# Four pairs of gate projections by Strassen's seven products in the second mixer, and two attention units to a block

## The chip, the cores and the metric

The kernel runs on one core of one Trainium2 chip. The metric is the device time of one execution in microseconds (us). Engines are called by their names in the profile: PE (matmuls), DVE (VectorE), ACT (ScalarE), POOL (GpSimd, which here mostly issues DMAs) and SP (which only issues DMAs).

## The reference, cut to what matters

Two transformer blocks follow each other on one sequence of 1024 tokens with 1024 channels. All arithmetic is float32. The change is in the first half of the second block:

```python
h = _rmsnorm(x, g_mix_pre)
proj = h @ w_in + b_in                      # 1024 -> 512 + 512 + 128 + 128 + 2048
u_pool, q, k, v, gates = jnp.split(proj, IN_SPLITS_2, axis=-1)
y_pool = _multiscale_pool(u_pool, w_pool, pool_scale)      # windows 2, 4, 8, 16
q, k = rotary on the first 16 of 64 channels of each head
y_attn = sliding-window attention with sinks (8 query heads, 2 key heads, window 128)
g = sigmoid(gates)                          # two gates of 1024 channels
merged = g_pool * (y_pool @ w_branch_pool) + g_attn * (y_attn @ w_branch_attn)
x = x + _rmsnorm(merged @ w_out, g_mix_post)
```

## The kernel before

Activations lie with channels on the 128 partitions and the 1024 tokens along the row. A projection is worked off in blocks: one block is 128 output channels, that is 8 slices of input channels, 2 halves of the tokens and 3 matmuls of 128x512 each, 48 matmuls in all. The three matmuls stand for one float32 product: operand and weight are each split into a high part in the fast float32 form (`fp32r`) and a low part, and high x high, low x high and high x low are added.

The input projection of the second mixer is 26 blocks, numbered by `d` (block `B_WIN2 + d`): first ten for queries, keys, values and pooling input, in the order `QKV_FIRST = (4, 5, 6, 7, 8, 9, 0, 1, 2, 3)` (four tiles of queries, one of keys, one of values, four for pooling), then the 16 gate blocks. The loops are written out by hand, one for each engine, and semaphores tie them. For each block:

- SP loads the weights into one of two slots of `w_stage`; ACT writes the high part `w_hi` (`next_high`, line L956); DVE writes the low part `w_lo` (`next_low`, L1729). Both are done in block `d` for block `d + 1`. PE waits for `w_lo` and for the evacuation of the block two before (`evac_done`).
- DVE evacuates the finished block from PSUM, multiplied by the norm's root `R` (L2770 for d < 10, L2774 for gates). For d < 10, ACT then adds the bias (`qkv_bias`, L1516). A gate block goes to `T` and from there by a DMA of POOL to `g_spill` in memory.

Rotary turning needs a copy of the query and key tiles in which groups of 8 partitions are swapped. POOL clears `swq` and `swk` by memset, then issues four DMAs for the queries (`swq<-Z`, 8 partitions x 4096 each) and four for the keys (L905). DVE then turns the queries in three instructions (`turn_queries`, L2699, L2701, L2703, one each in the blocks d = 4, 5, 6) and the keys (`turn_keys`, L2707 to L2710, d = 6).

Attention is cut into 16 units `u` (`UNITS`). The even and odd units use the two halves of the PSUM banks 4 to 7 in turn. Unit `u` belongs to block `d = 8 + u`: PE makes the scores (`scores2`, L3480) in the middle of the block, DVE shifts them and takes the maximum (`shift`, L2730 to L2739), ACT takes exponentials (`weights`, L1533), DVE normalises (`normalise2`, L2748 to L2752); in the middle of the next block PE transposes the weights (`turn_weights2`, L3489), ACT copies them (`turned_out`, L1523), at that block's end PE multiplies by the values (`values2`, L3499), and ACT copies the result out (`attended`, L1543). `scores2(u)` waits until `attended(u - 2)` has emptied its bank. DVE does the pooling of four tiles in the blocks `POOL_AT`, in one piece each.

Before it takes `X` for anything else, the kernel saves it to `x_spill` (4 MB, POOL).

The first mixer of the same kernel already has four pairs of its projection by Strassen's scheme: line L3026, 28 products of 12 matmuls each, 7 for a pair of blocks (`in_pair`, `in_low`, `in_out` and so on). Its loops are the ones that the change makes common.

## Time and profile before

| | |
|---|---|
| median of 3 runs | 2448.07 us (2447.64 to 2448.21) |
| the profiled execution | 2448.01 us, of which the span 2446.2 us |
| PE busy | 2411.3 us (99%) |
| DVE busy | 1735.8 us (71%) |
| ACT busy | 1074.3 us (44%) |
| mean granted TensorE clock | 0.997 |

Busy time is that in which an engine has an instruction in work. A matmul's length is modelled and overlaps with the next, so that the distance from start to start is the price of one. DMA issues stand at the engine that issues them.

### The profile page before, as it was taken

To read this page: it belongs to the slowest core of one execution; us is meant where nothing else is said; L and a number is where in the kernel's file an instruction comes from. 1 tells how busy PE (TensorE), PEld (TensorE's weight loads), DVE (VectorE), ACT (ScalarE), POOL (GpSimd) and SP (SyncE) were. 2 spreads that over 40 slices of the span, in tenths; PEclk is the share of its full clock that TensorE was granted. 3 is DMA by queue.
4 is the path that set the end of the run, shared out by engine and by line. 5 is a ranking of instruction groups with operands and counts; after the bars stand their busy time and mean duration, and the time that the engine had idled before them with its cause. 6 is when DMAs were issued, how large, how long until landed. Compare 5 with 4: busy or idle time off the path is not lost.

```text
span 2446.2 us, 29794 instructions
## 1 busy us (share of the span) xinstructions
PE 2411.3 (99%) x11510; PEld 1920.4 (79%) x11510; DVE 1735.8 (71%) x2088; ACT 1074.3 (44%) x1549; POOL 141.4 (6%) x230
## 2 busy tenths in 40 slices
PE   8999999999999999999999999999999999999997
PEld 6877666688888888888788777788878888888885
DVE  7668766646877778798863565455588777786888
ACT  7245777625333333333642333343456333334336
POOL 1002100000000010000001000000001000100001
PEclk9999999999999999999999999999999999999999
DMA  5110000132533382500133122234344433715103
GB/s 209 53 56 23 1 1 13 66 129 104 172 104 104 113 300 95 180 1 18 61 128 121 55 70 69 70 138 148 133 150 173 171 104 112 264 38 200 41 1 138
DMA packets 76231, 252.24 MB, mean 103 GB/s; under 512 B 6304, under 2 KB 6352, under 8 KB 76064
## 3 DMA queue, kind: packets, MB, share of 16 engines
q1 hardware_dynamic: 43728, 131.08, 16.6%
q0 software_dynamic: 32368, 119.32, 13.0%
q8 instruction: 88, 1.44, 0.2%
q14 instruction: 47, 0.39, 0.0%
HBM read 186.78 MB, written 62.91 MB: 102 GB/s over the span
## 4 chain that ended last, share of the span: by engine, by line
PE 87%; DVE 8%; ACT 2%; issue 2%; DMA 0%; DVEq 0%; ACTq 0%; SPq 0%; PEldq 0%
PE ps L2952 27%; PE ps L3385 20%; PE ps L3423 18%; PE ps L3553 7%; PE ps L3026 3%; PE ps L3256 2%; PE ps L3318 1%; DVE opQ_lo L2367 1%; DVE opQ_lo L2364 1%; PE ps L3298 1%; DVE spot L2409 1%; DVE ql_raw L2404 1%; PE ps L3480 1%; PE ps L3499 1%; PE ps L3220 1%
## 5 line engine op out<-in xcount | busy, mean ns | idle before, releaser
L3423 PE MATMUL ps<-opQ_hi 128*128 128x512 f32 x896 | 350.3, 391 | 2.8 <-DVE opQ_lo L2367 2.8
L3423 PE MATMUL ps<-opQ_lo,opQ_hi 128*128 128x512 f32 x896 | 348.7, 389 | 0.0
L3423 PE MATMUL ps<-opQ_hi,opQ_lo 128*128 128x512 f32 x896 | 348.7, 389 | 0.0
L3423 PEld LDWEIGHTS ps<-opQ_hi 128*128 128x128 f32 x896 | 168.2, 188 | 42.2 <-DVE opQ_lo L2367 7.2
L3423 PEld LDWEIGHTS ps<-opQ_hi,opQ_lo 128*128 128x128 f32 x896 | 168.2, 188 | 35.1
L3423 PEld LDWEIGHTS ps<-opQ_lo,opQ_hi 128*128 128x128 f32 x896 | 168.2, 188 | 34.6 <-issue 0.2
L1385 ACT ACTIVATE opQ_hi<-spot 128x1024 fp32r<-128x1024 f32 x80 | 84.9, 1061 | 235.8 <-PE ps L3423 196.7
L3385 PE MATMUL ps<-opQ_hi,form_hi 128*128 128x512 f32 x416 | 161.8, 389 | 0.0
L3385 PE MATMUL ps<-opQ_lo,form_hi 128*128 128x512 f32 x416 | 161.8, 389 | 0.0
L3385 PE MATMUL ps<-opQ_hi,form_lo 128*128 128x512 f32 x416 | 161.8, 389 | 0.0
L2952 PE MATMUL ps<-opP_hi,w_hi 128*128 128x512 f32 x510 | 159.5, 394 | 2.3 <-DVE T L2651 0.7
L2952 PE MATMUL ps<-opP_lo,w_hi 128*128 128x512 f32 x510 | 157.1, 389 | 0.0
L2952 PE MATMUL ps<-opP_hi,w_lo 128*128 128x512 f32 x510 | 157.1, 389 | 0.0
L2952 PE MATMUL ps<-opQ_hi,w_hi 128*128 128x512 f32 x480 | 155.6, 405 | 0.0
L1729 DVE TENSOR_TENSOR w_lo<-w_stage,w_hi 128x1024 fp32r<-128x1024 f32 x96 | 117.4, 1223 | 50.8 <-ACT w_hi L956 50.1
L2364 DVE TENSOR_TENSOR opQ_lo<-spot,opQ_hi 128x1024 fp32r<-128x1024 f32 x80 | 97.9, 1223 | 74.1 <-ACT opQ_hi L1385 74.1
L2952 PE MATMUL ps<-opQ_lo,w_hi 128*128 128x512 f32 x480 | 148.6, 391 | 0.0
L2952 PE MATMUL ps<-opQ_hi,w_lo 128*128 128x512 f32 x480 | 148.1, 390 | 0.0
L956 ACT ACTIVATE w_hi<-w_stage 128x1024 fp32r<-128x1024 f32 x96 | 100.9, 1051 | 86.9 <-PE ps L2952 59.0
L3385 PE MATMUL ps<-t_hi,form_hi 128*128 128x512 f32 x312 | 121.4, 389 | 0.0
L3385 PE MATMUL ps<-t_lo,form_hi 128*128 128x512 f32 x312 | 121.4, 389 | 0.0
L3385 PE MATMUL ps<-t_hi,form_lo 128*128 128x512 f32 x312 | 121.4, 389 | 0.0
(508 smaller groups left out, 4964.7 us busy)
## 6 DMA issues: line engine op xcount, KB each, us to landing
w_stage<-in_w_stream SPq DMA_DIRECT2D x96, 512.0 KB, 3.6
h_spill<-T POOLq DMA_DIRECT2D x56, 512.0 KB, 5.0
pair_raw<-in_w_stream SPq DMA_DIRECT2D x26, 1024.0 KB, 5.8
spot<-in_w_stream SPq DMA_DIRECT2D x24, 1024.0 KB, 7.2
spot<-h_spill POOLq DMA_DIRECT2D x24, 1024.0 KB, 9.3
qh_raw<-in_w_stream SPq DMA_DIRECT2D x8, 1024.0 KB, 11.6
ql_raw<-h_spill POOLq DMA_DIRECT2D x8, 1024.0 KB, 7.7
g_spill<-T POOLq DMA_DIRECT2D x16, 512.0 KB, 2.9
```

The lines of the kernel that those rows point to most:

```text
L956: act.activation(w_hi[:, slot, :], w_stage[:, slot, :], ACT.Copy).then_inc(w_hi_done, 1)
L1385: act.activation(weight_form(opQ_hi, i), source, ACT.Copy).then_inc(ff["form"], 1)
L1729: v.tensor_tensor(w_lo[:, slot, :], w_stage[:, slot, :], w_hi[:, slot, :].bitcast(F32), ALU.subtract)\
L2364: done(v.tensor_tensor(weight_form(opQ_lo, i), weight_form(ql_raw, i) if f == Q6 else weight_part(sc, name_w, g), weight_form(opQ_hi, i).b ...
L2367: done(v.tensor_tensor(inner_form(opQ_lo, i), t2_sum[:, :, :] if f == Q6 else inner_part(sc, name_h, g), inner_form(opQ_hi, i).bitcast(F32 ...
L2404: done(v.tensor_tensor(weight_form(ql_raw, i), weight_part(sc, "D", g), weight_part(sc, "A", g), ALU.subtract))
L2952: mm = pe.matmul(ps[:, psum + half, :], weight, operand[:, k, half * HALF:(half + 1) * HALF], start=(begin and x == 0 and weight is wh and ...
L3026: mm = pe.matmul(ps[:, (4 + f) % 8, :], weight[:, wcols(k)], operand[:, k0 + k, c0:c0 + HALF], start=(k == 0 and weight is form_h and oper ...
L3256: mm = pe.matmul(ps[:, bank, 0:n], QT[0:QKD, h, qt * P:(qt + 1) * P], KT[0:QKD, h, c:c + n], start=True, stop=True)
L3385: mm = pe.matmul(ps[:, pair_bank(x, p, j), :], weight[:, wcols(k)], operand[:, k0 + k, c0:c0 + HALF], start=(k == 0 and weight is form_hi[ ...
L3423: mm = pe.matmul(ps[:, down_bank(sc, f) + m, :], weight, operand, start=(g == 0 and kt == 0 and weight is wh and operand is hi), stop=(g = ...
L3553: mm = pe.matmul(ps[:, 2 * slot + half, :], weight[:, slot, wcols(k)], operand[:, k, c], start=(k == 0 and weight is w_hi and operand is h ...
```

## The change

Eight of the 16 gate blocks are taken out of the row of blocks and made as four pairs by Strassen's seven products: 28 products of 12 matmuls between block d = 5 and block d = 6. The row of blocks has 18 left (`MIX_BLOCKS`): six plain ones (`MIX_PLAIN`), then the products, then four for pooling input and eight gates. The sums of the operand's halves need `X`, scaled in place. The swapped copies and the turning come behind the products, since the products use the space of `swq`, `swk`, `tabC` and `tabS` (the cosine and sine tables). The units of attention stand two to a block, at `UNITS_AT`; pooling is cut into small parts that stand inside the units; the queries are turned in two halves, the second within unit 0.

```diff
-POOL_AT = (9, 11, 13, 15)
+MIX_PLAIN, MIX_PAIRS = 6, 4
+MIX_BLOCKS = 26 - 2 * MIX_PAIRS
+UNITS_AT = {8: (0, 1), 9: (2, 3), 10: (4, 5), 11: (6, 7), 12: (8, 9), 13: (10, 11), 14: (12, 13), 15: (14, 15), 16: (16,)}
+POOL_PARTS = [(gi, i) for gi in range(4) for i in range(gi + 2)]
+POOL_AT = {1: 1, 2: 1, 3: 1, 4: 1, 5: 1, 6: 1, 7: 2, 8: 2, 9: 2, 10: 2}
```

On POOL:

```diff
+            for p in range(MIX_PAIRS):
+                for slot in range(2):
+                    if p < MIX_PAIRS - 1 or slot == 0:
+                        gate_pair_out(p, slot)
+            pool.wait_ge(ff["mm"], MM0[1] + 7 * MIX_PAIRS)
+            pool.memset(swq[:, :, :], 0.0).then_inc(s["zero"], 1)
+            pool.wait_ge(s["zero"], 1)
+            pool.wait_ge(s["z"], 4)
+            for a in (0, 64):
+                for u, v in ((a, a + 8), (a + 8, a)):
+                    pool.dma_start(swq[u:u + 8, :, :], Z2[v:v + 8, 4:8, :]).then_inc(s["swap"], 16)
+            pool.dma_start(tabC[:, :], t["tabC"]).then_inc(s["consts"], 16)
+            pool.dma_start(tabS[:, :], t["tabS"]).then_inc(s["consts"], 16)
```

On ACT, ahead of and within the loop over the blocks:

```diff
+                if d == 1:
+                    for k in range(4):
+                        in_scaled(1, k)
+                elif d in (2, 3):
+                    in_sum_high(1, IN_SUMS[8 * (d - 2):8 * (d - 1)])
...
+                for u in units:
+                    if u:
+                        turned_out(u - 1)
+                    if u < UNITS:
+                        weights(u)
+                    if d < 10 and u == units[-1]:
+                        qkv_bias(d)
+                    if u:
+                        attended(u - 1)
```

On DVE:

```diff
+                if d == 2:
+                    in_sums(1, IN_SUMS)
+                elif d == 3:
+                    in_sum_lows(1, IN_SUMS[0:8])
...
+                elif d == 6:
+                    for third in range(3):
+                        turn_queries(0, third)
+                elif d == 7:
+                    turn_keys()
+                for u in UNITS_AT.get(d, ()):
+                    if u < UNITS:
+                        shift(u)
+                        if u == 0:
+                            turn_queries(1, 0)
+                        for _ in range(POOL_AT.get(u, 0)):
+                            pool_part(*POOL_PARTS[pooled])
+                            pooled += 1
+                        normalise2(u)
+                        if u == 0:
+                            turn_queries(1, 1)
+                            turn_queries(1, 2)
```

On PE:

```diff
+            def mixed_block(b, slot, units):
 
                 pe.wait_ge(w_lo_done, b + 1)
                 pe.wait_ge(evac_done, b - 1)
+                size = 4 if len(units) == 1 else 2
+                for k in range(0, DT, size):
+                    mm = product(2 * slot, slot, wcols, opQ_hi, opQ_lo, range(k, k + size), None, True, begin=(k == 0), end=(k + size == DT))
...
+                    u = units[k // (2 * size)]
+                    if k // size % 2:
+                        collect(u)
+                    else:
+                        attend(u)
...
+                elif u == 1:
+                    pe.wait_ge(s["rope"], 3)
...
+                if d == MIX_PLAIN - 1:
+                    pair_products(1)
```

`attend(u)` is `scores2(u)` and then `turn_weights2(u - 1)`; `collect(u)` is `values2(u - 1)` and, from unit 5 on, one matmul of pooling. `in_pairs` holds for each pair the splitting of its weights and the collecting of its seven products.

How the instructions stand on DVE from the turning to the first unit, before (blocks d = 4 to 8; `Z_137` is the projection's result, `[waits ...]` names the semaphores):

```order
L2770 TENSOR_TENSOR Z_137<-ps,R 128x1024 [waits mm_done]
L2699 TENSOR_TENSOR Z_137<-Z_137,tabC 128x4096 [waits swa_consts,swa_swap]
L1729 TENSOR_TENSOR w_lo<-w_stage,w_hi 128x1024 [waits w_hi_done,dve_step]
L2770 TENSOR_TENSOR Z_137<-ps,R 128x1024 [waits mm_done]
L2701 TENSOR_TENSOR swq<-swq,tabS 128x4096
L1729 TENSOR_TENSOR w_lo<-w_stage,w_hi 128x1024 [waits w_hi_done,dve_step]
L2770 TENSOR_TENSOR Z_137<-ps,R 128x1024 [waits mm_done]
L2703 TENSOR_TENSOR Z_137<-Z_137,swq 128x4096
```

And in the changed kernel, from the last product (d = 6) to the second half of the queries within unit 0 (d = 8):

```order
L1851 TENSOR_TENSOR w_lo<-w_stage,w_hi 128x1024 [waits w_hi_done,ff_mm]
L2831 TENSOR_TENSOR Z_144<-Z_144,tabC 128x2048 [waits swa_consts,swa_swap]
L2833 TENSOR_TENSOR swq<-swq,tabS 128x2048 [waits dve_step]
L2835 TENSOR_TENSOR Z_144<-Z_144,swq 128x2048 [waits dve_step]
L2933 TENSOR_TENSOR Z_144<-ps,R 128x1024 [waits mm_done]
L1851 TENSOR_TENSOR w_lo<-w_stage,w_hi 128x1024 [waits w_hi_done]
L2839 TENSOR_TENSOR Z_144<-Z_144,tabC 128x1024 [waits swa_swap]
L2841 TENSOR_TENSOR swk<-swk,tabS 128x1024
L2842 TENSOR_TENSOR kpad<-Z_144,swk 128x1024 [waits dve_step]
L2933 TENSOR_TENSOR Z_144<-ps,R 128x1024 [waits mm_done,swa_rope]
L1851 TENSOR_TENSOR w_lo<-w_stage,w_hi 128x1024 [waits w_hi_done]
L2863 SCALAR_TENSOR_TENSOR scw_151<-ps,mask_156 128x1024 [waits swa_consts,swa_vtc,swa_qk]
```

The three instructions on the queries stood behind the evacuation of a block, with a `w_lo` between them; now they stand ahead of the evacuation of block 6 and of the `w_lo` for block 8.

On POOL, before:

```order
L883 DMA x_spill<-X 128x8x1024 [waits x_upd]
L886 DMA tabC<-in_tabC 128x1024 [waits mm_done]
L887 DMA tabS<-in_tabS 128x1024
L895 MEMSET swk 128x1024
L897 MEMSET swq 128x4096
L905 DMA swq<-Z_137 8x4096 [waits swa_z,swa_zero]
```

and changed (`ff_mm` counts the products):

```order
L971 DMA g_spill<-gate_pair_111 128x1024 [waits swa_kept0,ff_relu]
L978 MEMSET swq 128x4096 [waits ff_mm]
L983 DMA swq<-Z_144 8x4096 [waits swa_z,swa_zero]
L983 DMA swq<-Z_144 8x4096 x3
L984 DMA tabC<-in_tabC 128x1024
L985 DMA tabS<-in_tabS 128x1024
```

The memset now waits for the last product, and the two tables come behind the copies.

On PE, at the first two units before (`kpad` and `Z_137` are keys and queries; eight more pieces of block 8 and half of block 9 stand where the dots are in the program):

```order
L3480 MATMUL ps<-kpad,Z_137 128x256 [waits swa_zero,swa_vtc,swa_rope]
...
L3489 MATMUL ps<-ident,scw_144 128x128 [waits swa_on]
L3489 MATMUL ps<-ident,scw_144 128x128 x7
L3480 MATMUL ps<-kpad,Z_137 128x256 x4
```

and changed:

```order
L3669 MATMUL ps<-kpad,Z_144 128x256 [waits swa_zero,swa_vtc,swa_rope]
...
L3669 MATMUL ps<-kpad,Z_144 128x256 [waits swa_rope]
L3669 MATMUL ps<-kpad,Z_144 128x256 x3
L3678 MATMUL ps<-ident,scw_151 128x128 [waits swa_on]
L3678 MATMUL ps<-ident,scw_151 128x128 x7
```

Between the scores of units 0 and 1 stood 48 matmuls; now 24 do, and the scores of unit 1 wait once more for the turning and stand ahead of the transposes of unit 0.

## Rows read from the trace of the kernel before

**Rows 1.** The page, busy time of engines and share of the span.

```profile
PE 2411.3 (99%) x11510; PEld 1920.4 (79%) x11510; DVE 1735.8 (71%) x2088; ACT 1074.3 (44%) x1549; POOL 141.4 (6%) x230
```

**Rows 2.** What PE waited for, longest first: total, times, longest.

```profile
PE ps L2952 <- DVE p_lo L1743: 8.5, 1, 8.5
```

**Rows 3.** Four stretches: length, then busy time (instructions) of PE, PEld, DVE, ACT, POOL.

```profile
84.00:158.00 74.00, 74.00 (x326) 59.83 (x324) 55.89 (x78) 20.19 (x31) 4.10 (x7) 1.00 0.15 46
1303.60:1314.48 10.88, 10.88 (x49) 9.01 (x48) 2.45 (x2) 2.10 (x2) 0.00 (x0) 1.00 0.15 48
1414.06:1428.42 14.36, 14.36 (x73) 10.95 (x73) 10.82 (x18) 4.53 (x13) 0.54 (x1) 1.00 0.20 73
1457.99:1473.19 15.20, 15.20 (x75) 11.34 (x75) 6.87 (x11) 5.22 (x14) 0.53 (x1) 1.00 0.21 71
```

**Rows 4.** Timeline of POOL: start, length, what it waited for.

```profile
1291.17 0.20 POOL L893 MEMSET kpad<- 128x128 f32 x1 [3.72 <-DMA x_spill<-X]
1292.35 3.54 POOL L897 MEMSET swq<- 128x4096 f32 x1
1317.49 2.03 POOL L905 DMA_DIRECT2D swq<-Z  x4 [21.60 <-ACT Z L1516]
```

**Rows 5.** DMA issues: KB each, median us from issue to landing.

```profile
w_stage<-in_w_stream SPq DMA_DIRECT2D x96, 512.0 KB, 3.6
```

**Rows 6.** The tile `swq`: landing of its four copies.

```profile
DMA to landing us min/median/max: 2.1/4.9/9.4
```

**Rows 7.** Timeline from the evacuation of block 2 to the weights of block 4.

```profile
1303.60 1.23 DVE L2770 TENSOR_TENSOR Z<-ps,R 128x1024 f32<-128x1024 f32 x1 [6.26 <-PE ps L2952]
1304.86 1.16 ACT L1516 ACTIVATE Z<-Z,col 128x1024 f32<-128x1024 f32 x1 [8.77 <-DVE Z L2770]
1305.92 1.04 ACT L956 ACTIVATE w_hi<-w_stage 128x1024 fp32r<-128x1024 f32 x1
1306.99 1.23 DVE L1729 TENSOR_TENSOR w_lo<-w_stage,w_hi 128x1024 fp32r<-128x1024 f32 x1 [2.17 <-ACT w_hi L956]
```

**Rows 8.** Timeline: turning of queries, of keys, and evacuation of block 7.

```profile
1328.49 4.43 DVE L2699 TENSOR_TENSOR Z<-Z,tabC 128x4096 f32<-128x4096 f32 x1 [1.91 <-DMA swq<-Z]
...
1352.60 1.22 DVE L2707 TENSOR_TENSOR Z<-Z,tabC 128x1024 f32<-128x1024 f32 x1
...
1356.25 1.23 DVE L1729 TENSOR_TENSOR w_lo<-w_stage,w_hi 128x1024 fp32r<-128x1024 f32 x1
1358.93 1.22 DVE L2770 TENSOR_TENSOR Z<-ps,R 128x1024 f32<-128x1024 f32 x1 [1.45 <-PE ps L2952]
1361.24 1.06 ACT L1579 ACTIVATE vpad<-ps 128x512 f32<-128x512 f32 x2
```

**Rows 9.** Timeline of unit 0, and the first transposes and values on PE.

```profile
1364.26 1.14 PE L3480 MATMUL ps<-kpad,Z 64*128 64x256 f32 x8
1365.44 1.23 DVE L2730 SCALAR_TENSOR_TENSOR scw<-ps,mask 128x1024 f32<-128x1024 f32 x1 [0.93 <-PE ps L3480]
...
1370.76 0.16 DVE L2748 TENSOR_TENSOR small<-small 128x4 f32<-128x4 f32 x1 [2.24 <-ACT small L1535]
1372.31 1.22 DVE L2770 TENSOR_TENSOR Z<-ps,R 128x1024 f32<-128x1024 f32 x1
1376.34 1.03 PE L3489 MATMUL ps<-ident,scw 128*128 128x128 f32 x8
1384.04 1.08 PE L3499 MATMUL ps<-ptw,vpad 128*64 128x256 f32 x8
```

**Rows 10.** Timeline of DVE, the first mixer's sums of operand halves.

```profile
39.89 0.69 DVE L1813 TENSOR_TENSOR in_t_raw<-X 128x512 f32<-128x512 f32 x1 [0.43 <-DMA pp_spill<-ppout]
43.76 0.68 DVE L1813 TENSOR_TENSOR in_t_raw<-X 128x512 f32<-128x512 f32 x1
```

**Rows 11.** Two stretches after PE's first wait, columns as above, then granted clock, DMA.

```profile
8.50:13.70 5.20, 5.20 (x12) 4.10 (x13) 3.43 (x3) 3.71 (x5) 0.00 (x0) 1.00 1.03 414
13.70:19.00 5.30, 5.30 (x24) 4.35 (x23) 5.23 (x6) 5.07 (x6) 0.65 (x1) 1.00 1.02 408
```

More of the change, by code:

```diff
@@ L889, in _ @@
-            pool.dma_start(wpool[:, :, :], t["w_pool"]).then_inc(s["consts"], 16)
+            for slot in range(2):
+                pair_spilled(pool, slot, MIX_PAIRS - 2)
+            pool.memset(swk[:, :], 0.0).then_inc(s["zero"], 1)
+            pool.wait_ge(s["zero"], 2)
+            pool.wait_ge(s["z"], 5)
+            pool.wait_ge(s["swap"], 64)
+            for a in (0, 64):
+                for u, v in ((a, a + 8), (a + 8, a)):
+                    pool.dma_start(swk[u:u + 8, :], Z2[v:v + 8, 8, :]).then_inc(s["swap"], 16)
@@ L890, in _ @@
+            gate_pair_out(MIX_PAIRS - 1, 1)
+            pool.memset(kpad[:, 0:P], 0.0).then_inc(s["zero"], 1)
+            pool.wait_ge(s["consts"], 32)
             pool.wait_ge(r_done, 4)
             pool.dma_start(mask2[:, :, :], t["mask2"]).then_inc(s["consts"], 16)
-            pool.wait_ge(s["spill"], 16 * DT + 16)
-            pool.memset(kpad[:, 0:P], 0.0).then_inc(s["zero"], 1)
+            pool.dma_start(icnt[:, :, :], t["icnt"]).then_inc(s["consts"], 16)
+            for slot in range(2):
+                pair_spilled(pool, slot, MIX_PAIRS - 1)
@@ L1880, in in_scale, with in_pairs @@
                 v.tensor_tensor(z, z, R[:, :], ALU.mult).then_inc(ff["relu"], 1)
+            def in_pairs(st):
+                last = PAIRS[st] - 1
+                for p in range(last + 1):
+                    more = p < last
+                    early = p < last - (0 if st else 1)
+                    if p:
+                        in_out(st, p - 1, 7)
+                        in_low(st, 7 * p + 2)
+                    in_low(st, 7 * p + 3)
+                    in_weight_sum(st, p, 3)
+                    if p:
+                        in_scale(st, p - 1, 1)
+                    in_low(st, 7 * p + 4)
+                    in_out(st, p, 1)
+                    in_low(st, 7 * p + 5)
+                    in_out(st, p, 2)
+                    in_low(st, 7 * p + 6)
+                    in_out(st, p, 3)
+                    if early:
+                        in_low(st, 7 * p + 7)
+                    in_out(st, p, 4)
+                    in_out(st, p, 5)
+                    if st == 0 and p < 2:
+                        in_rooted(3 - p)
+                    if early:
+                        for i in range(3):
+                            in_weight_sum(st, p + 1, i)
+                    in_out(st, p, 6)
+                    if more and not early:
+                        in_low(st, 7 * p + 7)
+                        for i in range(3):
+                            in_weight_sum(st, p + 1, i)
+                    if more:
+                        in_low(st, 7 * p + 8)
+                    in_scale(st, p, 0)
+                    if st == 0 and p < 2:
+                        in_rooted(1 - p)
@@ L2688, in pooled @@
[L2688 to L2703 removed]
+                else:
+                    head = pool_t[:, n % 2, 0:16]
+                    link(v.tensor_tensor(head, src[:, 0:16], icnt[:, gi, :], ALU.mult))
+                    v.tensor_tensor(u[:, 0:16], head, u[:, 0:16], ALU.subtract).then_inc(dve_step, 1)
+                    link.n += 1
+                    v.scalar_tensor_tensor(u[:, 16:S], src[:, 16:S], 1.0 / width, u[:, 16:S], ALU.mult, ALU.subtract)\
+                     .then_inc(s["pool"], 1)
+                    v.wait_ge(s["pool"], gi + 1)
+                    v.wait_ge(dve_step, link.n)
@@ new lines, in _, with turn_queries @@
+            two = [P, 2, S]
+            def turn_queries(half, third):
+                q_z, sw = Z2[:, 4 + 2 * half:6 + 2 * half, :], swq[:, 2 * half:2 * half + 2, :]
+                if third == 0:
+                    if half == 0:
+                        v.wait_ge(s["swap"], 64)
+                        v.wait_ge(s["consts"], 32)
+                    link(v.tensor_tensor(q_z, q_z, bc(tabC[:, :].unsqueeze(1), two), ALU.mult))
+                elif third == 1:
+                    link(v.tensor_tensor(sw, sw, bc(tabS[:, :].unsqueeze(1), two), ALU.mult))
+                else:
+                    v.tensor_tensor(q_z, q_z, sw, ALU.add).then_inc(s["rope"], 1)
@@ L3031, in gate_logits @@
+            pair_products(0)
             def gate_logits(pr):
```

570 lines of the change are left out of this document (301 added, 269 removed).

## The prediction

> **What bounds the kernel now.** I read the page first: PE is busy 99% of the span, DVE 71%, ACT 44% [rows 1]. Then the list of waits: PE's longest is 8.5 us at the very start, and between block 1 of the second mixer and the last unit PE waits for nobody [rows 2]. So each microsecond of matmuls taken from this stage is gained, and each wait of PE put in is lost. Then the stages by stretches: a plain block takes 10.88 us for 48 matmuls, 0.2267 us each; a block with one unit takes 14.36, with a pooling matmul 15.20 [rows 3]. A unit thus costs PE 3.48 us, or 4.32. DVE works 6.9 to 10.8 us in those blocks, with gaps.
>
> **What is removed.** Four pairs in plain form are 8 x 48 = 384 matmuls, by seven products 4 x 7 x 12 = 336. 48 fewer at 0.2267 us are **-10.9 us**. The same scheme runs in the first mixer without a wait of PE: 326 matmuls in 74.00 us, 0.227 us each, DVE busy 55.9 of 74.0 [rows 3]. Here DVE has the same work for each pair, so I cost the stage of products at its matmuls, 76.2 us.
>
> **What is added ahead of the products.** Sixteen sums on DVE stand in block 2. Six take 43.76 - 39.89 = 3.87 us [rows 10], so sixteen take 10.3. ACT first scales four tiles of `X` (4 x 1.1 us by [rows 7]), which must wait until `x_spill` has landed, 1291.2 in this trace [rows 4]: done 1295.5, bias 1 until 1296.6, `w_hi` of block 3 until 1297.6, its `w_lo` until 1298.8, sums until 1309.2. The evacuation of block 2 stands behind them, 5.6 us later than now, and from it to the start of block 4's `w_lo` it is 3.39 us [rows 7], then 1.2: ready at 1313.9, when PE wants it at 1314.48 [rows 3]. Cost 0, with 0.6 us of slack. The sixteen low parts (0.6 us each) fit in blocks 3 and 4 likewise.
>
> **What is moved behind the products.** Call E the end of the last product. PE starts block 6 at E + 1.15 (eight transposes, and the collecting of product 28); before, the transposes alone cost 0.95, so **+0.2 us**. Without a wait it would end block 7 at E + 1.15 + 21.76 = E + 22.9.
>
> The chain beside it starts on POOL. The memset of `swq` takes 3.54 us and now begins at E; the four copies follow about 0.5 later. In the trace the first is issued at 1317.49 and DVE, which waited for them, goes on at 1328.49, 11.0 later [rows 4, 8]. So they land at E + 15.1. Behind them stand `tabC` and `tabS`, 512 KB each, which before had been there long since; a load of this size takes 3.6 us [rows 5]. They add between 0 and 3.6; I take 1.5, as they use engines that the copies leave idle in part. DVE turns at **Q = E + 16.6**.
>
> DVE's queue now reads: three turns of half the queries, evacuation of block 6, `w_lo` of block 8, keys, evacuation of block 7, `w_lo` of block 9, unit 0. A turn over 4096 takes 4.43 us, over 1024 1.22 [rows 8], so over 2048 2.29: three are 6.9. From an evacuation through ACT's bias and `w_hi` to the next `w_lo` it is 3.39 [rows 7], plus 1.25: block 8's weights stand at Q + 11.45 = E + 28.05. **Wait 1** at block 8: 28.05 - 22.9 = **5.1 us**.
>
> From `w_lo` the evacuation of block 7 begins 1.15 + 3.65 later, behind the keys (1352.60 to 1356.25 [rows 8]), that is at Q + 15.0; from there to the end of ACT's two copies into `vpad` it is 1358.93 to 1362.3 [rows 8], 3.3 us: **V = Q + 18.3**. PE comes to the scores of unit 0 after a quarter of block 8, Q + 14.2. Before they stood after half. **Wait 2: 4.1 us.**
>
> The scores end at V + 1.1. DVE takes up unit 0 at V + 2.3, after `w_hi` and `w_lo` of block 9. From `shift` to `normalise2` it is 5.32 us now (1365.44 to 1370.76), to its end 6.87 (1372.31) [rows 9]. The first turn of the second half of the queries hides in the 2.24 us that DVE waits for ACT; the other two, 4.6, come behind: 11.5 us, at V + 13.8. PE makes 24 matmuls (5.44) and then wants the scores of unit 1, at V + 6.5. **Wait 3: 7.3 us.**
>
> In blocks 8 and 9 ACT's bias stands ahead of `attended(u - 2)`, and the bias waits for DVE's evacuation behind the block's second unit. From the end of the scores of unit 1 it is 0.1 + 6.87 + 1.25 + 1.06 + 0.3 = 9.6 us until that bank is free; PE gets there after transposes 0.96, 12 matmuls 2.72, values 1.08 and 12 matmuls again, 7.5 us [rows 7, 9]. **Wait 4: 2.1 us**, and **wait 5: 2.1 us** in the next block for the same reason. From block 10 on there is no bias and `attended` follows `weights`.
>
> In blocks 10 to 15 DVE has two units (13.7), pooling parts (1.3 each, of which 2.24 per unit are hidden; at most 0.6 over), an evacuation and a `w_lo` (2.3): 17 us. PE has 10.88 + 2 x 3.48 = 17.8, or 19.5 with pooling. PE stays the bound, cost 0; if it did not, each microsecond over would count six times.
>
> **Sum.** Waits 5.1 + 4.1 + 7.3 + 2.1 + 2.1 = 20.7; with -10.9 and +0.2 that is +10.0. One more term: after a long wait the matmuls may start slower. After PE's 8.5 us wait 12 matmuls take 5.20 us, then 24 take 5.30; the granted clock reads 1.00, the 2.4 GHz level, in both [rows 2, 11], so the column doesn't show it and the pitch does. Three waits here are of 4 to 7 us. Most of what that costs falls into the next wait; exposed are the scores of units 0 and 1 (1.1 each at most) and 1 us before wait 4: 0 to 3.3, I take **+1.0**. Result **+11.0 us** on the profiled execution's 2448.01 (its span is 2446.2), which is the median within 0.1: **2459.0 us**.
>
> The Trainium skill, TensorE: Matmul & The Clock Gate, says in Part 1 that an idle array falls back to 1.2 GHz and comes back when busy; the pitch in this trace agrees, the clock column doesn't. The Trainium skill, DMA: Bandwidth & Descriptors, says that a copy with 8 rows as its slowest dimension goes over 8 of the 16 engines ("How many engines"), and that descriptors of one queue on one engine start in order ("Two DMAs through the same engine are not ordered"). By it the tables would wait behind the copies where they share an engine and cost up to the whole 3.6 instead of 1.5, a sum of +13.1; no run here shows it.
>
> **Bounds.** Q at its earliest: memset and start 4.1, last issue 1.5 later, the median landing of 4.9 [rows 6] is E + 10.5; the second table, issued by E + 7.2, lands at E + 10.8. All waits together are Q - E + 4.1, so 14.9, and the result is +4.2: 2452. Latest: 15.1 + 3.6 = 18.7, and the clock's 3.3: 22.8 - 10.7 + 3.3 = +15.4, 2463.4.
>
> **Rivals.**
> - *Copies quicker than the trace (0.10).* The shortest landing is 2.1 us, and the four in the trace shared the engines with a load of weights. With 2.1 after the last issue and tables in 3, Q = E + 10: +3.4, 2451.4 to 2452.9, no change that can be told. Against: the tables are added to the same queue, and a load of weights falls there again.
> - *All hidden, faster (0.07).* If the turning ended before PE needs it, 2437.3. It decides at waits of 10.7 in all, Q = E + 6.6. For it: the same turning cost PE nothing before. Against: memset 3.5, issue 2.0 and shortest landing 2.1 make 7.6, without tables. It would need a wait that I misread, such as wait 3.
> - *The slack ahead of the products breaks (0.10).* SP now loads 1 MB for a pair just before the 4 MB of `x_spill`. At the 414 GB/s of [rows 11] that is 2.5 us later for the spill, so 1.9 at block 4: 2461.
> - *DVE becomes the bound in the blocks with two units (0.07).* With 1 us over in each of six, 2465. For it: 17 of 17.8 us in block 10. Against: 2.5 us free where pooling runs.
>
> **How the numbers follow.** The forecast has 0.66. Its own bounds are 2452 to 2463.4; with the slack's rival inside, **2452 to 2464** leaves out the faster case, most of the last and part of the quick copies, under 2 in 10. A measurement can tell 0.2% (4.9 us): faster 0.07, same 0.10, slower 0.83.
>
> **What would show it.** The products' line should have 28 x 12 matmuls in 76.2 us without a wait. The list of PE's waits should show, in this order of time: matmul after DVE `w_lo` (5), scores after ACT `vpad` (4), scores after DVE's turned queries (7), and twice scores after ACT's copy of the result (2). The timeline should show the first turn 15 to 18 us after E behind DMAs. Wrong it is if the turn starts before E + 10, if PE comes to the scores of unit 1 without a wait, or if the products wait.

## The result and the profile after

The changed kernel takes 2462.95 us (median of 4 runs, 2461.21 to 2463.71) against 2448.14 for the one before: 1.0057 times as long, 95% interval 1.0043 to 1.0071, slower by 14.8 us. The profiled execution took 2461.21 us, 13.2 over that of before; its span is 2459.5 against 2446.2.

The page's busy line, which answers to [rows 1]:

```profile
PE 2407.7 (98%) x11462; PEld 1914.6 (78%) x11462; DVE 1792.4 (73%) x2187; ACT 1097.6 (45%) x1593; POOL 141.6 (6%) x230
```

PE has the 48 matmuls fewer that the change promised, and yet only 3.6 us less busy time. The list of what PE waited for, which answers to [rows 2] (total, times, longest):

```profile
PE ps L3115 <- DVE w_lo L1851: 8.9, 3, 7.3
PE ps L3115 <- DVE p_lo L1865: 8.5, 1, 8.5
PE ps L3669 <- DVE Z L2835: 3.9, 1, 3.9
...
PE ps L3669 <- issue: 2.5, 1, 2.5
...
PE ps L3669 <- ACT X L1647: 1.9, 1, 1.9
```

Only the 8.5 was there before. Where the new ones lie is in PE's timeline (start, length, instruction, in brackets the idle time ahead and what ended it):

```profile
1315.32 0.73 PE L3115 MATMUL ps<-opQ_hi,w_hi 128*128 128x512 f32 x2 [1.05 <-DVE w_lo L1851]
...
1414.58 0.73 PE L3115 MATMUL ps<-opQ_hi,w_hi 128*128 128x512 f32 x2 [0.17 <-DVE gate_pair L2000]
...
1443.97 1.22 PE L3115 MATMUL ps<-opQ_hi,w_hi 128*128 128x512 f32 x2 [7.34 <-DVE w_lo L1851]
...
1450.96 2.08 PE L3669 MATMUL ps<-kpad,Z 64*128 64x256 f32 x8 [2.54 <-issue]
...
1464.69 2.08 PE L3669 MATMUL ps<-kpad,Z 64*128 64x256 f32 x8 [3.95 <-DVE Z L2835]
1466.70 1.97 PE L3678 MATMUL ps<-ident,scw 128*128 128x128 f32 x8
...
1476.48 1.14 PE L3669 MATMUL ps<-kpad,Z 64*128 64x256 f32 x8
...
1496.15 1.14 PE L3669 MATMUL ps<-kpad,Z 64*128 64x256 f32 x8 [1.91 <-ACT X L1647]
```

These are the first matmuls of block 4, 6 and 8, and the scores of units 0, 1, 2 and 4. The wait at unit 0 has no cause beside it (`issue`). ScalarE's row shows one: `vpad`'s copies end 0.1 us before those scores.

```profile
1449.80 1.06 ACT L1704 ACTIVATE vpad<-ps 128x512 f32<-128x512 f32 x2
```

The idle time ahead of blocks 4 and 8 and of the units sums to 1.05 + 7.34 + 2.54 + 3.95 + 1.91 = 16.8 us. The span grew by 13.3; with the 10.9 saved and 0.2 spent, 24.0 us were lost, so 7.2 do not show as idle time but as slow matmuls: scores that took 1.14 in [rows 9] take 2.08, transposes 1.97 for 1.03. Three stretches of PE, columns as in [rows 3] and [rows 11]:

```profile
1337.20:1413.37 76.17, 76.17 (x337) 63.02 (x336) 53.61 (x76) 20.60 (x33) 3.50 (x7) 1.00 0.23 83
```

```profile
1443.90:1448.30 4.40, 4.33 (x12) 3.24 (x12) 4.33 (x5) 0.00 (x0) 0.00 (x0) 0.64 0.42 119
...
1464.60:1476.40 11.80, 11.71 (x48) 8.54 (x48) 6.88 (x12) 4.59 (x13) 0.00 (x0) 0.73 0.00 0
```

The first is the whole stage of products, without a gap. In the other two, behind the waits of 7.34 and 3.95, the granted clock is 0.64 and 0.73: partly at the 1.2 GHz level.

Last, the chain that the wait at block 8 hangs on. POOL, then DVE (start, length, what it waited for):

```profile
1413.61 3.54 POOL L978 MEMSET swq<- 128x4096 f32 x1
1417.45 2.02 POOL L983 DMA_DIRECT2D swq<-Z  x4 [0.29 <-POOL swq L978]
1419.46 0.55 POOL L984 DMA_DIRECT2D tabC<-in_tabC  x1
1420.03 0.54 POOL L985 DMA_DIRECT2D tabS<-in_tabS  x1
1420.56 0.97 POOL L988 MEMSET swk<- 128x1024 f32 x1
1430.76 2.00 POOL L994 DMA_DIRECT2D swk<-Z  x4 [9.23 <-DMA swq<-Z]
```

```profile
1432.45 2.29 DVE L2831 TENSOR_TENSOR Z<-Z,tabC 128x2048 f32<-128x2048 f32 x1 [15.53 <-DMA tabS<-in_tabS]
...
1442.69 1.23 DVE L1851 TENSOR_TENSOR w_lo<-w_stage,w_hi 128x1024 fp32r<-128x1024 f32 x1 [2.16 <-ACT w_hi L1054]
```

Call E the end of the last product, 1413.37 here, and Q the start of the first turn, as the prediction does. POOL sees the copies landed at E + 17.4 and goes on to `swk`; the first turn comes at Q = E + 19.1, when `tabS` has landed. The landings of the four copies, which answer to [rows 6]:

```profile
DMA to landing us min/median/max: 2.8/5.0/11.2
```

The slowest took 11.2 us, against 9.4 before. The last was issued at 1419.0, so they had landed by 1430.2, E + 16.8.

### The profile page after: what moved, and what is told of

Same layout as the page of the kernel before. It is cut to its first block, busy times and chain, and to the rows that moved or that the text cites. A ratio compares the mean times of both kernels' runs of the same rounds, so it can differ in the third digit from the quotient of the medians.

```text
span 2459.5 us, 29949 instructions
## 1 busy us (share of the span) xinstructions
PE 2407.7 (98%) x11462; PEld 1914.6 (78%) x11462; DVE 1792.4 (73%) x2187; ACT 1097.6 (45%) x1593; POOL 141.6 (6%) x230
## 3 DMA queue, kind: packets, MB, share of 16 engines
q0 software_dynamic: 32368, 119.32, 13.1%
## 4 chain that ended last, share of the span: by engine, by line
PE 82%; DVE 11%; ACT 3%; issue 2%; DMA 1%; POOL 0%; DVEq 0%; ACTq 0%; SPq 0%; PEldq 0%; POOLq 0%
PE ps L3553 20%; PE ps L3115 20%; PE ps L3591 18%; PE ps L3735 6%; PE ps L3192 6%; PE ps L3424 2%; PE ps L3486 1%; DVE opQ_lo L2496 1%; DVE opQ_lo L2493 1%; PE ps L3466 1%; DVE spot L2538 1%; PE ps L3669 1%; DVE ql_raw L2533 1%; DMA x_spill<-X 1%; PE ps L3678 1%
## 5 line engine op out<-in xcount | busy, mean ns | idle before, releaser
L1851 DVE TENSOR_TENSOR w_lo<-w_stage,w_hi 128x1024 fp32r<-128x1024 f32 x88 | 107.5, 1222 | 48.2 <-ACT w_hi L1054 47.8
L1054 ACT ACTIVATE w_hi<-w_stage 128x1024 fp32r<-128x1024 f32 x88 | 92.6, 1053 | 96.1 <-PE ps L3115 58.9
L3115 PE MATMUL ps<-opQ_hi,w_hi 128*128 128x512 f32 x352 | 117.9, 416 | 8.6 <-DVE w_lo L1851 8.4
L3115 PEld LDWEIGHTS ps<-opP_hi,w_hi 128*128 128x128 f32 x510 | 94.9, 188 | 24.9 <-issue 2.4
L3115 PEld LDWEIGHTS ps<-opP_lo,w_hi 128*128 128x128 f32 x510 | 95.7, 188 | 20.0
```

The lines of the kernel that those rows point to most:

```text
L1054: act.activation(w_hi[:, slot, :], w_stage[:, slot, :], ACT.Copy).then_inc(w_hi_done, 1)
L1851: v.tensor_tensor(w_lo[:, slot, :], w_stage[:, slot, :], w_hi[:, slot, :].bitcast(F32), ALU.subtract)\
L3115: mm = pe.matmul(ps[:, psum + half, :], weight, operand[:, k, half * HALF:(half + 1) * HALF], start=(begin and x == 0 and weight is wh and ...
```

## The experiments

Unless said otherwise each is the changed kernel with one edit. E and Q are read in each trace as above.

### Copies issued before the last products

```diff
+            pool.wait_ge(ff["mm"], MM0[1] + 7 * (MIX_PAIRS - 1) + 2)
             pool.memset(swq[:, :, :], 0.0).then_inc(s["zero"], 1)
...
+            gate_pair_out(MIX_PAIRS - 1, 0)
+            pool.wait_ge(ff["mm"], MM0[1] + 7 * MIX_PAIRS)
             pool.dma_start(tabC[:, :], t["tabC"]).then_inc(s["consts"], 16)
```

> The memset of swq and its four copies now wait for product 23 (the last that reads the place of swq), 13.6 us ahead of the end E of the last product; the two tables still wait for E. Theory (the chain of memset, copies, tables and turning sets PE's first three waits): copies have landed by E + 2, tables by E + 6, so the first turn starts at E + 6 instead of E + 19; the waits at block 8 and at the scores of unit 0 go, that at the scores of unit 1 stays (about 6 us, since DVE can take unit 0 only after its scores), and little more: 2449 to 2451 us. Rival (two units to a block, or the products' work on DVE, is the cause): over 2458 us, with waits of PE elsewhere.

(The place left out holds the four copies.) Measured: 2452.87 us (ratio 1.0016, interval 1.0006 to 1.0025), 10 less than the changed kernel. PE's timeline, scores of units 0, 1, 2 and 4:

```profile
1441.25 1.14 PE L3670 MATMUL ps<-kpad,Z 64*128 64x256 f32 x8 [2.35 <-issue]
...
1454.88 2.08 PE L3670 MATMUL ps<-kpad,Z 64*128 64x256 f32 x8 [6.82 <-DVE Z L2836]
...
1466.66 1.13 PE L3670 MATMUL ps<-kpad,Z 64*128 64x256 f32 x8 [0.37 <-ACT X L1648]
...
1486.34 1.14 PE L3670 MATMUL ps<-kpad,Z 64*128 64x256 f32 x8 [1.91 <-ACT X L1648]
```

E is 1412.92 and the first turn starts at 1422.74, Q = E + 9.8. Block 8 no longer waits. The scores of unit 0 start 28.3 after E instead of 37.6: Q came 9.3 earlier, and so did they. The wait at unit 1 did not shrink, it rose to 6.8, as PE comes there without slow matmuls and the turn of the second half stands as long behind unit 0 as it did. The turn had been expected at E + 6; it came later because `tabS` took 8.5 us to land, and the time lies 2 to 4 above the 2449 to 2451 expected.

### Tables issued ahead of the memset and the copies

```diff
+            pool.dma_start(tabC[:, :], t["tabC"]).then_inc(s["consts"], 16)
+            pool.dma_start(tabS[:, :], t["tabS"]).then_inc(s["consts"], 16)
             pool.memset(swq[:, :, :], 0.0).then_inc(s["zero"], 1)
...
-            pool.dma_start(tabC[:, :], t["tabC"]).then_inc(s["consts"], 16)
-            pool.dma_start(tabS[:, :], t["tabS"]).then_inc(s["consts"], 16)
```

> The tables are issued at E, ahead of the memset and the copies. Theory (tables add to the end of the copies' queue, about 2.2 us of the trace): the copies start 1.1 us later, the turn starts about 1 to 2 us earlier, 2461 to 2462 us. Rival (the engines' total work counts, in whatever order): no change, 2463.

Measured: 2458.55 us (1.0042, 1.0027 to 1.0056), 4.4 less. The first turn waits for the copies now, at 1430.31 with E = 1413.81: Q = E + 16.5, 2.6 earlier. The wait at block 8 fell by the same 2.6, to 4.76; the others stayed (2.58, 4.00, 1.91). So the tables behind the copies cost the changed kernel 2.6 of its Q. It is made of three parts: the copies are issued 1.3 later (E + 5.3), DVE goes on 11.2 after their first issue, as in [rows 4, 8], where they took 12.8 in the changed kernel, and nothing stands behind them, where `tabS` came 2.2 later. The medians differ by 4.4, the spans of the profiled executions by 2.2 (2457.3), as Q does; the rest the trace does not show.

### ScalarE's bias behind attended

```diff
-                    if d < 10 and u == units[-1]:
-                        qkv_bias(d)
                     if u:
                         attended(u - 1)
                     if 0 <= u - 5 < 8:
                         pooled_out(u - 5)
+                    if d < 10 and u == units[-1]:
+                        qkv_bias(d)
```

> In blocks 8 and 9 ACT's bias stands behind the copy of the attention's result instead of ahead of it. Theory (the bias behind DVE's evacuation holds the bank): the wait of 1.9 us at the scores of unit 4 goes, the one at unit 2 is covered by slow matmuls already: 2460.5 to 2461.5. Rival (the bank is free early and PE waits for DVE's units): no change.

Measured: 2459.76 us (1.0047, 1.003 to 1.0063), 3.2 less. The wait of 1.91 at unit 4 is gone (a later 0.46 and 0.33 came), and units 1 to 2 stand 10.85 apart instead of 11.79. From unit 1 to unit 4 that is 28.56 against 31.46, 2.9 less, and the time lies 0.7 below the range expected. Nothing changed ahead of unit 1: block 8 waits 7.30, and the scores of units 0 and 1 stand 13.62 apart (13.73).

### The memset made twice

```diff
             pool.memset(swq[:, :, :], 0.0).then_inc(s["zero"], 1)
             pool.wait_ge(s["zero"], 1)
+            pool.memset(swq[:, :, :], 0.0).then_inc(s["zero"], 1)
+            pool.wait_ge(s["zero"], 2)
```

> The memset of swq is done twice, 3.5 us more on POOL at E. Theory (the chain from POOL is the path): the first turn starts 3.5 us later and all of it arrives, 2466 to 2467. Rival (PE's waits come from DVE's own load): no change, 2463.

Measured: 2463.54 us (1.0065, 1.0048 to 1.0081). The copies are issued 3.6 later after E, but the turn only 2.4 later (Q = E + 21.45): from the first copy's issue to the turn it is 13.8 us here and 15.0 in the changed kernel. The wait at block 8 rose by 2.4, to 9.70. I had expected 2466 to 2467. The median rose by 0.6 alone, which by itself would fit the rival; the profiled execution (span 2461.6) stands 2.1 over that of the changed kernel. The trace shows the delay arriving, at the turn, at block 8 and at the scores of unit 0; the times can't settle 2 us between two medians of 4 runs.

### Tables in a place that is free before the last product

Added to the early copies: the lower halves of two sums change places, and the tables lie where one of them had been, which is free after product 24.

```diff
-        tabC, tabS = at("tabC", [P, S], PB + 40), at("tabS", [P, S], PB + 44)
+        tabC, tabS = at("tabC", [P, S], PB + 8), at("tabS", [P, S], PB + 12)
```

> Edit: swq's memset and its four copies stand as in the run of the early copies (behind product 23), and the two tables get a home that is free before the last product (the addresses of the sums' lower halves change places, tabC and tabS lie where the lower half of the first sum was) and are issued behind product 24, so the first turn needs to wait only for VectorE to end the pair's sums. Theory (a chain of waits with several ends): once the first turn is ahead of what block 8 needs, an earlier turn buys nothing. The first turn comes at E+3 to E+5 (it was E+9.8 with early copies alone, E+19.1 in the changed kernel). Block 8 waits 0, scores of unit 0 wait 0.5 to 2.4 (vpad's copies stand behind the bias of block 7), scores of unit 1 still 6 to 8 (the second half of the queries is still turned behind unit 0's normalising), unit 4 1.9, block 4 1.0: time 2450 to 2453, against 2452.9 with early copies alone. Rival (the turn's time is worth its full length at any place): 6 us earlier give 6 us, 2447. Rival (something else than these waits, such as VectorE's load in blocks of two units): no change from 2453 and the waits move to later units.

Measured: 2451.99 us (1.0012, 1.0002 to 1.0021), 0.9 below the early copies. Q is E + 4.1 (1419.32, E = 1415.25), 5.7 earlier, and the scores of unit 0 start at 1442.09, E + 26.8, 1.5 earlier. The scores of unit 0 still wait 0.87, now for a chain that starts at PE's own block 7: its evacuation, the bias, `vpad`. An earlier Q buys nothing once PE arrives no sooner, and the rival that any microsecond of Q is worth a microsecond fell. The ten times lie in two groups, 2450.2 to 2451.0 and 2453.0 to 2453.7, so that the 0.9 between medians says little; the distances from E say it.

### All waits of the trace taken away by order

The kernel of the run above, and three changes of order: the second half of the queries is turned in block 6 behind the first, `vpad`'s copies stand ahead of block 7's bias, and the bias of blocks 8 and 9 behind `attended`.

```diff
                     for third in range(3):
                         turn_queries(0, third)
+                    for third in range(3):
+                        turn_queries(1, third)
...
-                        if u == 0:
-                            turn_queries(1, 1)
-                            turn_queries(1, 2)
```

> Edit: the run with the tables elsewhere, and three changes of order: the second half of the queries is turned in block 6 right behind the first half (not around unit 0), vpad's two copies on ScalarE stand ahead of the bias of block 7, and ScalarE's bias stands behind attended and pooled_out. Theory (all that the change lost beside its 10.9 us of matmuls are these waits and the slow matmuls that follow them): block 8, units 0, 1, 4 wait 0 to 1 in all, block 4 keeps its 1.0; with no idle time there is no stretch of half-speed matmuls either: time 2448.1-10.9+0.2+1.0+(0 to 2) = 2438.5 to 2441, faster than the kernel before. Rival (blocks with two units are bound by VectorE, 73% busy over the span): the transposes of unit 0 to 2 wait 2 to 5 each for the normalised weights, time 2443 to 2448. Rival (the lower clock comes from the products or from elsewhere, not from the idle time): granted clock in 1436 to 1476 stays under 0.9, time 2444 to 2446.

Measured: 2444.61 us (0.9982, 0.9973 to 0.9992), below the kernel before, 4 to 6 us above what I expected and within the rival's 2443 to 2448. PE's timeline:

```profile
1439.47 1.14 PE L3666 MATMUL ps<-kpad,Z 64*128 64x256 f32 x8 [0.16 <-DVE kpad L2844]
1446.20 1.14 PE L3666 MATMUL ps<-kpad,Z 64*128 64x256 f32 x8
...
1450.98 1.60 PE L3675 MATMUL ps<-ident,scw 128*128 128x128 f32 x8 [3.65 <-DVE scw L2887]
```

The waits named are gone, and one of 3.65 stands in their place: the transposes of unit 0 want the normalised weights. DVE had `w_lo` of block 9 ahead of unit 0's shift (1442.84), while the scores were ready at 1440.6. That is the rival's wait, but at unit 0 alone; the later units waited 0.46 and 0.32. So the rival was right about one place of DVE's order, and not about the load of the blocks. The other rival fell: the granted clock from 1436 to 1476 is 0.96 with the waits gone and 0.74 in the changed kernel, so the lower clock went with the idle time.

### The order alone, copies and tables where they were

Of the run above only the three changes of order. That of `vpad`, a move up in the body of ScalarE's loop:

```diff
+                if d == 7:
+                    for w in range(2):
...
                 if d < 10 and not units:
                     qkv_bias(d)
```

> Edit: the three changes of order alone (second half of the queries in block 6, vpad's copies ahead of the bias of block 7, bias behind attended); copies and tables as in the changed kernel, so that the first turn stays at E+19. Theory (the chain behind the first turn is as long as what stands in it): six more us of turning now stand ahead of evacuation 6, so block 8 waits 7.3+6.9 = 14.2 (13 to 15), unit 0 0 to 2, units 1 and 4 nothing: the sum stays 15 to 18 and the time 2460 to 2464, no gain, though three waits are gone. Rival (each of the waits is a cost of its own and the order removes it): 2463-3.9-1.9 = 2457.

Measured: 2458.36 us (1.0039, 1.0024 to 1.0053).

```profile
1450.98 1.22 PE L3112 MATMUL ps<-opQ_hi,w_hi 128*128 128x512 f32 x2 [14.06 <-DVE w_lo L1851]
...
1455.53 1.13 PE L3664 MATMUL ps<-kpad,Z 64*128 64x256 f32 x8
...
1462.30 1.14 PE L3664 MATMUL ps<-kpad,Z 64*128 64x256 f32 x8
...
1466.02 1.09 PE L3673 MATMUL ps<-ident,scw 128*128 128x128 f32 x8 [2.59 <-DVE scw L2885]
```

The wait at block 8 is 14.06, where 14.2 was worked out. Idle time up to unit 4 is 18.4 us, more than the changed kernel's 16.8, yet the span is 3.2 shorter: one long wait leaves one slow start (8 matmuls until 1454.5, 1.7 us over their pitch), the changed kernel's three waits behind each other left slow matmuls up to 1471. I had expected 2460 to 2464, by adding waits alone; the rival's 2457 is as near, but its mechanism is not what the rows show, as block 8 waits for all that was moved there.

### The pair's load behind the loads of blocks 2 and 3

```diff
-            gate_pair_in((MIX_PAIRS - 1) % 2)
             for i in range(2, MIX_PLAIN):
                 win2_in(i)
+                if i == 3:
+                    gate_pair_in((MIX_PAIRS - 1) % 2)
```

> Edit: SP issues the load of the first turned pair (1 MB into T) behind the loads of blocks 2 and 3 of the second mixer instead of ahead of them, so that it is not in flight beside the 4 MB spill of X, all else as in the changed kernel. Theory: the spill lands 1 to 3 us earlier (it landed at 1292.5 and ScalarE waited 2.9 for it), the sums and with them evacuation 3 and the split of block 4's weights come earlier, and block 4's wait of 1.05 goes to 0 (0 to 0.3): time 2461.9, 1 below the changed kernel, which the trace shows and the times hardly. Rival (the spill is as slow without it, or VectorE's sums are what is late): the wait stays at 1.0.

Measured: 2462.99 us (1.0058, 1.0041 to 1.0074). Block 4's wait is 1.35, not 0. The issues of the two transfers (KB, us to landing), in this run:

```profile
x_spill<-X POOLq DMA_DIRECT2D x1, 4096.0 KB, 17.8
T<-in_w_stream SPq DMA_DIRECT2D x1, 1024.0 KB, 13.6
```

The spill started at 1276.8 and the load at 1280.8: it still ran beside the spill. The edit did not separate them, so this run says nothing against the theory; the run below keeps them apart with a wait.

### All of it, the load behind the spill, and the shift ahead of the weights

```diff
                 elif in_turned(p):
                     sp.wait_ge(x_upd, DT)
+                    sp.wait_ge(s["spill"], 16 * DT + 16)
...
+                    if d != 8:
+                        next_low(b, None, slot)
...
                         shift(u)
+                        if u == 0:
+                            next_low(b, None, slot)
```

(The load's place is behind block 2's.)

> Edit: the run with all waits taken away, and two changes more. SP's load of the first turned pair waits until the spill of X has landed (and stands behind the load of block 2), so that the two are never in flight together; VectorE makes the lower half of block 9's weights behind unit 0's shift instead of ahead of it, in the time in which it waited 2.24 for ScalarE's exponentials. Theory: the transposes of unit 0, which waited 3.65 for the normalised weights in that run, wait 0 to 0.5; the spill lands 1 to 3 us earlier and block 4's wait of 1.05 goes; so the second mixer has under 1 us of waits and no slow matmuls, and the time is that of the kernel before less the 10.9 us of matmuls: 2436.5 to 2438.5. If only the shift's place helps (the run of the load behind blocks 2 and 3 left block 4's wait at 1.35, but its load was still in flight beside the spill): block 4's wait stays at 1.0 and the time is 2437.5 to 2440. Rival (blocks of two units are bound by VectorE): the wait moves to the transposes of units 1 to 3, 2 to 4 us, and the time stays over 2442.

Measured: 2438.84 us (0.9962, 0.9948 to 0.9976): 9.6 faster than the kernel before, 24 faster than the changed one.

```profile
x_spill<-X POOLq DMA_DIRECT2D x1, 4096.0 KB, 13.2
```

```profile
1438.80 1.14 PE L3671 MATMUL ps<-kpad,Z 64*128 64x256 f32 x8
...
1445.53 1.13 PE L3671 MATMUL ps<-kpad,Z 64*128 64x256 f32 x8
...
1447.00 1.09 PE L3680 MATMUL ps<-ident,scw 128*128 128x128 f32 x8 [0.33 <-DVE scw L2889]
...
1454.79 1.14 PE L3671 MATMUL ps<-kpad,Z 64*128 64x256 f32 x8
...
1473.27 1.13 PE L3671 MATMUL ps<-kpad,Z 64*128 64x256 f32 x8
```

The spill lands in 13.2 us (15.8 in the kernel before, 17.5 in the changed one), ScalarE waits no more for it, and block 4 starts without a wait. The 15.8 was not that of a store alone either: before, `tabC` and `tabS` (1 MB) were issued right behind the spill and landed 15.9 and 16.0 us after their issues; the change took them away from there and put the pair's 1 MB beside it. The 3.65 is 0.33. From 1300 to 1520 PE waits 1.7 us in all. The products, the pairs and the two units to a block are all still there: these waits, and the slow matmuls behind them, are what had stood against the 10.9 us.

### The waits filled with matmuls

```diff
+            def keep_busy(count):
+                for _ in range(count):
+                    pe.matmul(ps[:, 6, :], opQ_hi[:, 0, 0:P], opQ_hi[:, 1, 0:HALF], start=True, stop=True)
```

with 28 ahead of block 8, and 8 and 14 ahead of the scores of units 0 and 1.

> Edit: the changed kernel with 28, 8 and 14 matmuls (128x512, operands opQ, into bank 6, their result is not used) put ahead of block 8, of unit 0's scores and of unit 1's scores, where TensorE waited 7.34, 2.54 and 3.95; at the pitch of 0.227 they take 6.35, 1.81 and 3.17 us, less than each wait. They add work and take no wait's cause away. Theory (some 7 of the 14.8 us that the changed kernel lost are slow matmuls, and these follow from TensorE's idle time): granted clock 0.95 to 1.00 from 1436 to 1476, matmuls at 0.227 and scores at 1.14 behind the waits, time 2455.5 to 2459, 4 to 7 below the changed kernel though TensorE does 11.3 us more work. Rival (slow matmuls come from something else in these blocks, such as the 64-row scores or the load of weights; or the loss is only the waits): 2462 to 2463, or later by what the fillers overshoot.

Measured: 2462.26 us (1.0057, 1.004 to 1.0074), as the changed kernel. The stretch of PE at block 8's first quarter, and the scores of units 0, 1 and 2:

```profile
1444.50:1447.40 2.90, 2.81 (x12) 2.35 (x13) 2.87 (x4) 0.00 (x0) 0.00 (x0) 1.00 0.59 164
```

```profile
1451.58 1.67 PE L3677 MATMUL ps<-kpad,Z 64*128 64x256 f32 x8 [2.16 <-issue]
...
1465.20 1.64 PE L3677 MATMUL ps<-kpad,Z 64*128 64x256 f32 x8 [2.06 <-DVE Z L2835]
...
1476.55 1.13 PE L3677 MATMUL ps<-kpad,Z 64*128 64x256 f32 x8 [0.85 <-ACT X L1647]
```

Half of my theory held: with PE busy through most of the wait (1.04 is left), the clock reads 1.00 at block 8, where it was 0.64, and the twelve matmuls take 2.81 us for 4.33. It did not hold everywhere: behind waits of 2.16 and 2.06 that were left, the scores of units 0 and 1 take 1.67 and 1.64 (2.08 in the changed kernel), not the 1.14 expected. The other half, that this is worth 4 to 7 us, fell: the time is the rival's. The scores of unit 1 start at E + 51.3 (E = 1413.90) in both kernels, because they follow DVE's turn and not PE. What PE no longer lost in slow matmuls it waited. Behind unit 1 the start of unit 2's scores follows the end of unit 1's by 9.71 us in both kernels, so only the length of unit 1's own scores counts there (2.08 for 1.14, 0.9 us). The 7.2 us of slow matmuls in the changed kernel are mostly not a cost beside the waits but a part of the same gap.

## Why the prediction was right, and where it was off

Slower, by 14.8 where 11.0 was forecast, 2462.95 in a range of 2452 to 2464. The mechanism was the one described, with each of its five waits in its place. That the time stayed 1 us inside the range was in part luck: Q lay outside its own bounds (19.1, latest 18.7), and block 4's wait was not in the sum, but of the 3.3 us that the upper bound held for the clock only about 1.0 came. The steps, each against the traces:

**The removed matmuls** cost what they should: 336 in 76.17 us without a gap, 76.2 forecast. Block 6 starts at E + 1.2 (1.15). Both right.

**The chain behind Q** was right to 0.2 us, and runs that move Q show that it is a chain. The starts of the scores of units 0 and 1, from their rows:

| run | Q - E | scores 0 after Q | scores 1 after scores 0 |
|---|---|---|---|
| forecast | 16.6 | 18.3 | 13.8 |
| changed kernel | 19.1 | 18.5 | 13.7 |
| copies early | 9.8 | 18.5 | 13.6 |
| tables first | 16.5 | 18.5 | 13.7 |
| memset twice | 21.5 | 18.5 | 13.6 |
| waits filled | 19.2 | 18.5 | 13.6 |
| bias behind attended | 19.1 | 18.5 | 13.6 |
| load behind 2 and 3 | 19.7 | 18.5 | 13.7 |
| tables elsewhere | 4.1 | 22.8 | 13.6 |
| order alone | 19.0 | 22.9 | 6.8 |
| all waits | 4.2 | 21.9 | 6.7 |
| all, two more | 4.2 | 21.9 | 6.7 |

In the order of the changed kernel the 18.5 does not move while Q goes over 12 us; then PE's own block 7 takes over. With the tables elsewhere the scores of unit 0 come at E + 26.8, so Q counts until E + 8.3 (the terms of the forecast, 22.9 + 2.7 - 18.3, give E + 7.3). The three runs with another order have other distances, as the second half's turns stand ahead of unit 0 there.

This also shows an error in the rival "all hidden". It put the point at which nothing is lost at Q = E + 6.6, by the rule that all waits are Q - E + 4.1. The rule ends where waits 1 and 2 end; waits 3, 4 and 5, 11.5 together by the forecast's own figures, do not depend on Q and are over the 10.7 gained. The tables elsewhere put Q at E + 4.1, and the kernel was still slower than before (2451.99, interval from 1.0002). Only the runs that changed the order as well were faster.

**Q itself is the mis-sized term**: 16.6 forecast, 19.1 measured. The memset took its 3.54 and the copies were issued at E + 4.1; from there they took 12.8 us to land where the trace of before had 11.0, and the tables came 2.2 behind them (1.5 forecast). So 1.8 of the 2.5 us lie in the copies and 0.7 in the tables. The 11.0 was carried over from a trace in which no table stood behind the copies; that the tables would slow the copies themselves was put at nothing. One pair of runs, with the copies at the same distance from E, shows that they do: the slowest copy lands after 9.7 us with the tables elsewhere (issued behind the copies) and after 8.4 with the copies early (tables not yet issued). The rest of the 1.8 is open: the slowest landing is 11.2 in the changed kernel, 9.5 with the tables first, where the copies also start 1.3 later, but 9.9 with the memset twice, where they start 3.6 later with the tables behind them as before. So the moment counts as well, and what ran beside them at it was not varied.

The Trainium skill, DMA: Bandwidth & Descriptors, says under "Two DMAs through the same engine are not ordered" that descriptors of one queue on one engine start in order; the prediction took from it tables that wait up to 3.6 behind the copies, an estimate of +13.1 in all. They came 2.2 behind, between that and the 1.5. That the profiled execution shows +13.2 comes from other terms as well, the slower copies and block 4. Which engine held which transfer was not tried.

A smaller slip: from Q to block 8's weights the terms sum to 11.5 (6.9 + 3.39 + 1.25), not 11.45; measured are 11.5.

**The waits.** In distances between scores, so that slow matmuls count where they lie (against the run with all of it and two more, whose few waits are taken off where they lie):

| place | forecast | measured |
|---|---|---|
| to the scores of unit 0 (waits 1, 2) | 9.2 | 37.6 - 26.1 = 11.5 |
| unit 0 to 1 (wait 3) | 7.3 | 13.7 - 6.7 = 7.0 |
| unit 1 to 2 (wait 4, clock) | 2.1 + 1.0 | 11.8 - 8.9 = 2.9 |
| unit 2 to 4 (wait 5) | 2.1 | 1.9 |
| block 4 | 0 | 1.05 |
| sum | 21.7 | 24.3 |

(8.9 is 9.26 less the 0.33 waited there; the 1.9 from unit 2 to 4 is 19.67 less 18.48, with 0.66 waited in the latter.) Wait 3 reads 3.95 in the list of waits and wait 4 reads nothing, since PE came late by its own slow matmuls; the distances show that both are there. From the end of unit 1's scores to the start of unit 2's it is 9.7 in every run with the bias in its place (9.6 forecast), and the scores' own length adds 0.9: the forecast's 2.1 + 1.0, within 0.2. ACT's bias as the cause of waits 4 and 5 is shown by the run that moved it, with 2.9 us less from unit 1 to unit 4; PE then has no wait between units 1 and 2, and the 1.9 that stays there is slow matmuls. `vpad` and the turn were moved in one run, all waits taken away against the tables elsewhere: 0.87 at unit 0 became 0.16, and 13.6 became 6.7. That `vpad` belongs to the first and the turn to the second is read from the rows and was not tried one by one.

**The slack of 0.6 us ahead of the products** broke: block 4 waited 1.05. It had a chance of 0.10, at 1.9 us, for the reason that came about: the spill of `X` landed in 17.5 us instead of 15.8. That the pair's load beside it is the cause is shown by the run that kept them apart, 13.2. The rival's price, 2.5 us for one MB more, was that of a load added; here 1 MB (the tables) had gone as 1 MB came, and the spill still landed 1.7 later. Counting this term at nothing was an error of 1.05.

**DVE in blocks of two units** was no bound: PE's waits at units 2 to 8 in the fastest run are at most 0.44.

Of the terms missed, the place ahead of unit 0 (Q) is 2.3 and block 4 is 1.05; the other waits came out 0.7 lower. Together 2.6, where the spans say 2.3 (24.0 less 21.7); the 0.3 between them is not placed. The median of the runs lies 1.7 above the profiled execution, which no step explains.

## What to carry to other kernels

Work taken from the bound engine is gained only if what stands beside it is moved too. Here the change lost 14.8 us while a memset and six DMAs started only when the last product had ended. With these started earlier the loss was about 3 (tables elsewhere), and with five more pieces of work in another place (the second half's turns, `vpad`, the bias, one `w_lo`, the pair's load) the 48 matmuls were worth 9.6. Ask of each small preparation that hides beside a long stage where it stands once the stages change places. And measure a suspected chain by distances between two events over several runs, not by the list of waits: a wait can be shorter than its cause when the engine arrives late by itself.

## What the runs showed that I had not expected

- After a wait of 7.3 us the twelve matmuls of block 8 took 4.33 us instead of 2.81, at a granted clock of 0.64; with the same wait filled by 28 matmuls the clock stayed 1.00. The Trainium skill, TensorE: Matmul & The Clock Gate, Part 1, says that an idle array falls back to 1.2 GHz and comes back when busy; these rows agree. At the start of the program twelve matmuls took 5.20 us with 1.00 in the column [rows 11]; no run here shows whether that has the same cause.
- Behind one wait of 14.06 us the matmuls took 1.7 us over their pitch and were back at it 3.5 us later. Behind waits of 7.34, 2.54 and 3.95, which ended within 21 us, 7.2 us were lost in slow matmuls, and they came back to their pitch 6 us after the last wait (1471 in PE's timeline).
- One 4 MB store took 13.2 us when SP's only loads beside it were those of 0.5 MB, 15.8 with two tables and some small loads (1.3 MB) behind it in its own queue, and 17.5 and 17.8 with a 1 MB load beside it as well, whether that was issued ahead of the store or 4 us into it.
- Four copies of 8 partitions, 128 KB each, took 12.8 us from the first issue to the last landing, and `tabS`, 512 KB, behind them 12.3, where a load of weights of that size has a median of 3.7. With the tables ahead of them the copies took 11.2.
